# Moving the index path of a sparse attention beside the input projection, and its last top-k into the attention

## The reference

```python
(cq, k_att, v_att, k_idx, w_idx, q_m, k_m, v_m, o_m, i_m, f_m) = split(h @ w_in)   # 256, 512, 512, 64, 8, 4 x 512, 4, 4
cq = rms_norm_2(cq, q_latent_norm)
q = rope(cq @ w_q_up)            # 8 heads of 64
q_idx = rope(cq @ w_qidx_up)     # 8 index heads of 64
k, k_idx = rope(k_att), rope(k_idx)
# per block of 128 queries:
idx_score = sum over the 8 index heads of relu(q_idx . k_idx) * w_idx    # causal
sel = top_k(idx_score, 128)
att = softmax attention of q over the selected keys
# then an mLSTM on q_m, k_m, v_m, o_m, i_m, f_m, the product with w_out, and a SwiGLU
```

## Time and profile before

| | us |
|---|---|
| median of 3 runs | 3909.8 (3907.99 to 3910.78) |
| profiled execution, its own time | 3912.18 |
| its span | 3910.4 |
| PE busy / DVE busy / ACT busy / POOL busy, of the span | 90% / 45% / 28% / 0% |
| mean granted clock of TensorE | 0.932 of full |
| DMA queue of SP, share of 16 engines | 27.6% |

### The profile page before, as it was taken

The page is one execution under the profiler, slowest core; times in us unless marked ns, Lnnn a source line. Parts: engine busy times, 40 slices in busy tenths (PEclk is TensorE's granted clock), DMA queues, the critical chain, the costliest instruction groups (busy, mean ns, idle before and its releaser), DMA issues. The chain is left out here.

```text
span 3910.4 us, 49122 instructions
## 1 busy us (share of the span) xinstructions
PE 3521.6 (90%) x20384; PEld 2898.7 (74%) x20384; DVE 1753.6 (45%) x3310; ACT 1092.7 (28%) x1782; POOL 10.7 (0%) x12
## 2 busy tenths in 40 slices
PE   6998999999999988999998974799999983799997
PEld 5987677888887976878876963468887872568886
DVE  3225554333334235644344447653333448654333
ACT  3112443111113222532223222531222322533222
POOL 0000000000000000000000000000000000000000
PEclk9996999999999987999999995899999996799999
DMA  5440102423331210144442310026443320013332
GB/s 191 128 151 1 47 23 63 130 97 99 108 115 44 76 55 26 34 149 149 148 143 91 92 53 0 1 71 194 146 143 113 87 77 0 1 44 92 97 97 70
DMA packets 318717, 336.52 MB, mean 86 GB/s; under 512 B 12024, under 2 KB 233760, under 8 KB 318496
## 3 DMA queue, kind: packets, MB, share of 16 engines
q1 hardware_dynamic: 318496, 333.38, 27.6%
HBM read 329.67 MB, written 3.67 MB: 85 GB/s over the span
## 5 line engine op out<-in xcount | busy, mean ns | idle before, releaser
L1528 DVE TENSOR_TENSOR weights_low<-weights,weights_high 128x1024 fp32r<-128x1024 f32 (+4 forms) x424 | 485.7, 1148 | 1211.3 <-ACT weights_high L1155 1209.5
L1155 ACT ACTIVATE weights_high<-weights 128x1024 fp32r<-128x1024 f32 (+4 forms) x424 | 421.3, 996 | 1383.7 <-PE banks L580 956.2
L987 PE MATMUL banks<-h_high,weights_high 128*128 128x512 f32 (+1 forms) x1760 | 659.8, 375 | 10.1 <-DVE h_low L1540 6.0
L987 PE MATMUL banks<-h_low,weights_high 128*128 128x512 f32 (+1 forms) x1760 | 650.8, 370 | 0.0
L987 PE MATMUL banks<-h_high,weights_low 128*128 128x512 f32 (+1 forms) x1760 | 649.5, 369 | 0.0
L580 PE MATMUL banks<-weights_high,h_high 128*128 128x426 f32 (+3 forms) x1424 | 519.0, 364 | 4.2 <-DVE h_low L1540 4.2
L580 PE MATMUL banks<-weights_high,h_low 128*128 128x426 f32 (+3 forms) x1424 | 510.4, 358 | 0.0
L580 PE MATMUL banks<-weights_low,h_high 128*128 128x426 f32 (+3 forms) x1424 | 509.7, 358 | 0.0
L987 PEld LDWEIGHTS banks<-h_high,weights_high 128*128 128x128 f32 x1760 | 333.3, 189 | 79.3 <-issue 18.4
L987 PEld LDWEIGHTS banks<-h_high,weights_low 128*128 128x128 f32 x1760 | 333.4, 189 | 56.4
L987 PEld LDWEIGHTS banks<-h_low,weights_high 128*128 128x128 f32 x1760 | 333.7, 190 | 51.6
(11 more groups left out here) (257 smaller groups left out, 3908.2 us busy)
## 6 DMA issues: line engine op xcount, KB each, us to landing
projected<-in_w_mod SPq DMA_DIRECT2D x80, 1024.0 KB, 5.3
weights<-in_w_gate_up SPq DMA_DIRECT2D x88, 512.0 KB, 3.9
weights<-in_w_down SPq DMA_DIRECT2D x80, 512.0 KB, 3.7
weights<-in_w_in SPq DMA_DIRECT2D x80, 426.0 KB, 3.4
weights<-in_w_gate SPq DMA_DIRECT2D x44, 512.0 KB, 6.5
weights<-in_w_up SPq DMA_DIRECT2D x44, 512.0 KB, 6.3
weights<-in_w_mod SPq DMA_DIRECT2D x32, 512.0 KB, 3.8
weights<-in_w_out SPq DMA_DIRECT2D x32, 512.0 KB, 3.6
```

The source lines that it names most:

```text
L987: mm = pe.matmul(bank[:, 0:cnt], wt[:, k, :], x[:, k, a:a + cnt], start=(k == 0 and q == 0), stop=(k == KD - 1 and q == 2))
L1155: act.activation(WH[s_ % 2][:, 0:k * n], slots[j % LAND][:, 0:k * n], ACT.Copy).then_inc(S["w_high"], 1)
L1528: dve.tensor_tensor(WL[s_ % 2][:, 0:k * n], slots[split_of[s_] % LAND][:, 0:k * n], WH[s_ % 2][:, 0:k * n].bitcast(F32), ALU.subtract).the ...
```

## The change

The two layers of the second kind are reordered in five ways; the arithmetic is the same.

1. The columns of w_in are reordered on the host: cq, index keys, index weights and gates come first (336 columns), then keys, values and the mLSTM's four. The projection has 7 chunks, of 336 and six times 512 columns: 28 slots. ACT copies all of its banks (`keeps`).
2. The index path moves beside the projection. PE does, in its side banks behind the unit of the slot: the turns of cq (slot 6), of the index keys (7), the products with w_qidx_up for tiles 1 to 3 (8, 9), the turns of the index queries (11 to 13), the index scores of tile 1 (14, 15: eight matmuls of 256 keys), of tile 2 (16 to 19: two heads each) and of tile 3 (20 to 23). DVE does the norm of cq (4, 5), the rope of index keys (6) and index queries (10 to 12), the sums of tile 1 (15, 16), the 16 rounds of tile 1 (17 to 20, four each) and 15 rounds of tile 2 (22 to 26, three each; the last one behind the projection). ACT takes the relu, two a slot, in slots 15 to 24, into four buffers.
3. POOL takes over: the rope of the keys (four tiles), the weighted sums of tiles 2 and 3 (16 heads, a scale and an add each), and the rope of the queries (four tiles, six instructions of 128x256 each), in that order.
4. After the projection are left: the product with w_q_up, the turns of keys and queries, and the attention.
5. The 16 rounds of tile 3 stand in DVE's list between the pairs of the attention: two rounds behind the `weigh` of each of pairs 0 to 7, the mask behind pair 8. PE no longer waits for `nearly_chosen`, and does 3 instead of 5 dummy matmuls there.

The diff, cut to its core:

```diff
-M_Q, M_K, M_V, M_O, M_I, M_F = 1352, 1864, 2376, 2888, 3400, 3404
+A_C, A_KI, A_WI, M_I, M_F = 0, 256, 320, 328, 332
+W_IN2_FIRST = 336
...
-        chunks = [(W // 8 * j, W // 8, IN_T) for j in range(8)]
+        chunks = [(0, W_IN2_FIRST, IN_T)] + [(W_IN2_FIRST + 512 * j, 512, IN_T) for j in range(6)]
...
+            if second and slot == 8:
+                cols(w["w_qidx_up"], 0, 512, 0, 2, split=False)
...
+                elif 16 <= slot < 24:                                  # PE
+                    n = 2 if slot < 20 else 3
+                    for h in (2 * (slot % 4), 2 * (slot % 4) + 1):
+                        bank = side.fill(pe, "a")
+                        pe.matmul(bank[:, 0:128 * (n + 1)], QIT[b:b + 64, n - 1, f, :], KIT[b:b + 64, 0:128 * (n + 1)],
+                                  start=True, stop=True).then_inc(S["side"], 1)
...
-                if second:
-                    pe.wait_ge(S["nearly_chosen"], 1)
-                    warm(5, 6)
-                else:
-                    warm(3, 6)
+                warm(3, 6)
...
+                pe.wait_ge(S["key_rope_pool"], 1)
                 for f in range(4):
                     turn_columns(lambda t: pr(t, A_K + 128 * f, 128), ["a"])
+                for n in range(LAT_T):
+                    pe.wait_ge(S["query_rope"], n + 1)
+                    bank = B.fill(pe, "a")
...
+                def rotate(x, n):                                      # POOL
+                    pool.tensor_tensor(t1, x1, s_, ALU.mult)
+                    step(pool.tensor_tensor(t2, x2, s_, ALU.mult))
+                    pool.tensor_tensor(x1, x1, c, ALU.mult)
+                    step(pool.tensor_tensor(x2, x2, c, ALU.mult))
+                    pool.tensor_tensor(x1, x1, t2, ALU.subtract)
+                    step(pool.tensor_tensor(x2, x2, t1, ALU.add))
...
+                        part = RL[g % 4][:, 0:nk]
+                        if h == 0:
+                            pool.tensor_scalar(total[:, 0:nk], part, WI[:, n, h:h + 1], None, ALU.mult)
+                        else:
+                            step(pool.tensor_scalar(part, part, WI[:, n, h:h + 1], None, ALU.mult))
+                            pool.tensor_tensor(total[:, 0:nk], total[:, 0:nk], part, ALU.add)
...
+                for n in range(LAT_T):
+                    pool.wait_ge(S["emptied_act"], n + 1)
+                    rotate(QQ[:, n, :], n)
+                    pool.sem_inc(S["query_rope"], 1)
...
+                if 4 <= q < 8:                                         # ACT, before relu q
+                    act.wait_ge(S["index_sum"], q // 2 - 1)
+                elif q >= 8:
+                    act.wait_ge(S["pool_sum"], q - 7)
+                kept(RL[q % 4][:, 0:n], bank[:, 0:n], 1.0, ACT.Relu)
...
+                elif 17 <= slot < 21:                                  # DVE
+                    choose(1, 4 * (slot - 17), 4 * (slot - 16))
...
+                elif 22 <= slot < 27:
+                    choose(2, 3 * (slot - 22), 3 * (slot - 21))
...
+                    if between:
+                        between(p)
...
+                def last_tile(p):
+                    if p < 8:
+                        choose(3, 2 * p, 2 * p + 2)
+                    elif p == 8:
+                        mask(3)
```

More of the change, by code:

```diff
@@ L321, in layer @@
                     unit(w["w_mod"][PT * k:PT * (k + 2), 512 * c:512 * (c + 1)].rearrange("(k p) n -> p k n", p=PT), 2, 512, split=False)
+            if second and slot == 8:
+                cols(w["w_qidx_up"], 0, 512, 0, 2, split=False)
     if second:
-        for n in ("w_q_up", "w_qidx_up"):
-            cols(w[n], 0, 512, 0, 2, split=False)
+        cols(w["w_q_up"], 0, 512, 0, 2, split=False)
     else:
@@ L518, in layer @@
     turn = "ad"
+    keeps = "aa" if second else turn
     def by_rows(f, bank, h):
@@ L1162, in modulate @@
                         bank = T.share(act)
-                        act.activation(HH[:, f, a:a + cnt], bank[:, 0:cnt], ACT.Identity, scale=AT[:, which, f, r:r + 1],
+                        act.activation(HH[:, f, a - GOFF:a - GOFF + cnt], bank[:, 0:cnt], ACT.Identity, scale=AT[:, which, f, r:r + 1],
                                        bias=MT[:, 2 * which, f, r:r + 1]).then_inc(S["h_high"], 1)
@@ new lines, in choose @@
+            def choose(n, r0, r1):
+                nk = 128 * (n + 1)
+                sums = SUMS[n][:, 0:nk]
+                if r0 == 0:
+                    if n > 1:
+                        dve.wait_ge(S["pool_sum"], 8 * (n - 1))
+                    step(dve.tensor_tensor(sums[:, nk - 128:nk], sums[:, nk - 128:nk], CN[:, C_CAU:C_CAU + 128], ALU.add))
+                for r in range(r0, r1):
+                    src = sums if r == 0 else WK[:, 0:nk]
+                    step(dve.max(m8, src))
+                    step(dve.match_replace(WK[:, 0:nk], m8, src, TAKEN))
@@ L1828, in _, with mask @@
+            def mask(n):
+                nk = 128 * (n + 1)
+                mk = MK[:, MKO[n]:MKO[n] + nk]
+                step(dve.tensor_scalar(mk, WK[:, 0:nk], TAKEN, NEG, ALU.is_gt, ALU.mult))
+                step(dve.tensor_tensor(mk[:, nk - 128:nk], mk[:, nk - 128:nk], CN[:, C_CAU:C_CAU + 128], ALU.add))
             for j, (a, n, tt) in enumerate(chunks):
@@ L1837, in _ @@
                         side.empty(dve, "a", "d")
-                    if second and (j, i) != (7, 3):
+                    if second:
                         beside_projection(j, i)
@@ L1842, in _ @@
                 for i, t in enumerate(tt):
-                    bank = PB6.empty(dve, turn[i % 2], "d")
+                    bank = PB6.empty(dve, keeps[i % 2], "d")
                     if bank is not None:
                         dve.tensor_copy(pr(t, a, n), bank[:, 0:n]).then_inc(S["kept_dve"], 1)
-            PB6.all_emptied(dve)
+            if not second:
+                PB6.all_emptied(dve)
             if start_loads:
```

345 lines of the change are left out of this document (203 added, 142 removed).

## The result

The changed kernel takes 3782.79 us (median of 4 runs, 3782.15 to 3783.39), the kernel before 3909.04 us (4 runs): a ratio of 0.9677, with a 95% interval of 0.966 to 0.9693. Forecast was 3789, 6 us more. The profiled span is 3780.4 us, 130.0 less than the 3910.4 of before.

What follows compares the result with a forecast made beforehand. DVE's chain of relu sums and selection was taken to bound the kernel between projection and attention. Per layer 89.9 - 9.0 - 1.4 + 2.6 - 21.5 = 60.6 us, 121.2 for two, from 3909.8 to 3789; range 3760 to 3835.

Steps and rivals of the forecast that it cites:

- five terms: Per layer: 89.9 us gained before the attention, 9.0 and 1.4 lost in it, 2.6 gained and 21.5 lost in the projection.
- Stage A: From the projection's last matmul to the attention's first turned pair: 120.4 us becomes 30.5, a gain of 89.9 a layer.
- Rival (a): Query ropes and index sums: POOL takes 1.4 us an instruction with strided reads; 3830 us; chance 15%.
- The estimate of 0.56 us: Query ropes: a POOL instruction of 256 takes 0.56 us, the four ropes are 4 us shorter, the sum 3781.
- Projection: Input projection, per layer: 2.6 us gained by reordered columns, 21.5 lost to PE's added index work, no new wait.
- POOL's sums: Index sums beside the projection: scale 1.0 and add 1.5 us, 2.5 a head, 5.0 of the 6.2 two heads have.
- Rival (c): Beside the projection: DVE and POOL exclude each other, splits wait in ten slots; 12 us a layer, 3813; chance 10%.
- Stages B and C together: Attention pairs 0 to 7 lose 9.0 us a layer with DVE as bound; pairs 8 to 15 lose 1.4.
- Clock in C: Attention pairs 8 to 15: clock taken as the mean of the two layers, since nothing changes there.
- Rival (b): Attention pairs 8 to 15: clock stays at 1.2 GHz throughout, 19 us above the mean, 3827; chance 12%.
- (d): Ropes and pairs 8 to 15: POOL is as fast as DVE and the clock rises with pair 8; 3768; chance 11%.
- (e): Projection: POOL's sums hold ACT, ACT's splits hold PE; slower than before, 3967 at three times the POOL prices; chance 2%.

## Why the prediction was right, point by point

The time was 6 us off, and the signs of all five terms were right. By its steps, per layer, forecast against measured (layer 3, layer 4):

- **Stage A**, forecast 30.5 us: 30.5 and 30.3. Inside it, POOL's instruction was put at 0.7 us between the bounds 0.42 and 1.0, and took 0.72; the tile 4.4 against 4.5; the last rope T + 21.0 against T + 21.4. What chose 0.7 over the copy's rate was that the earlier trace rows showed a copy beside DVE work; the trace now has the copy at 3.96 us again beside that work and the ropes at 0.72 without. Rival (a), POOL at 1.4 us, is out. The estimate of 0.56 us for 256 elements, worked out in proportion from the figure for 2048 in the Trainium skill (GPSIMD Engine Reference, section 3.1), was too low: the instruction took 0.72, and no run here has one of 2048 elements with two inputs. That the kernel came out near the 3781 us of that estimate is luck, from the terms below.
- **Projection**, forecast 18.9 us lost: 17.4 and 17.5. The columns were right: the matmul of 336 columns has its 0.154 us pitch. The scores took 9.8 where the earlier trace rows had given 10.0. Two terms were too high: the products with w_qidx_up took 4.3 and not 5.3, and the changes of operand some 2 and not 3.4; the turns, 3.8 and not 2.8, made up for a part. No wait of PE was foreseen and none came beyond the one at the start (1.9 us) that was there before (2.10).
- **POOL's sums**, forecast 1.0 and 1.5 us (scale and add) at 512 keys: 1.56 and 1.28. The total of 2.5 us a head became 2.8 undisturbed and 3.2 in the mean, since in every second head the scale began during a split of DVE and took 2.1 to 2.35. The shares were wrong too: the instruction with one tensor and a scalar per partition is the dearer one, though it reads one input less. The cover of four buffers was enough, and the run with two more instructions a head shows by how much.
- **Rival (c)**, DVE and POOL excluding each other beside the projection: the exclusion exists and cost PE no wait. In the changed kernel's layer 3, a POOL scale that began during a split (2273.81 to 2275.33), and a POOL add during which a split began:

```profile
2274.41 2.35 POOL L1209 TENSOR_SCALAR scratch<-scratch,small 128x512 f32<-128x512 f32 x1 [0.16 <-POOL scratch L1210]
...
2286.81 1.28 POOL L1210 TENSOR_TENSOR scratch<-scratch,projected 128x512 f32<-128x512 f32 x1
```

```profile
2287.29 1.89 DVE L1642 TENSOR_TENSOR weights_low<-weights,weights_high 128x1024 fp32r<-128x1024 f32 x1 [1.40 <-ACT weights_high L1248]
```

  The add ends at 2288.09, and the split 1.1 us behind it, at 2289.18; undisturbed a split is 1.23. Of the step that priced this rival, "every split waits for a POOL add (1.5) in ten slots, and uses up its 2.9 of slack where DVE is full", the wait was over-priced and the slack was not used up: the mean split was 1.30 us where an undisturbed one is 1.23, and PE's slots had room. It was mostly POOL that waited. The Trainium skill (SBUF — State Buffer, "Who interferes with whom") has the rule that a DVE instruction with two SBUF inputs contends with a GpSimd instruction that reads SBUF, and the trace agrees here too.
- **Stages B and C together**, forecast 9.0 + 1.4 = 10.4 us lost: 7.5 and 13.1, 10.3 in the mean. The sum was right and the parts were not, by three steps, and that it came out so close is in part luck: the three runs that leave the attention as it is had B and C together 2.3 us shorter in the mean. One: I counted eight pairs of DVE work between the turns of pair 0 and pair 8. DVE's chain, from its first copy at 2333.12 to its last round at 2367.3, is 34.2 us, close to the forecast's; but pair 8 turns 2.4 us before it ends, so B shows a loss of 5.3 and 6.1 and the rest falls in C. Two: a pair took 3.65 us with 128 keys and 4.1 with 256, where the forecast had 3.95 and 4.4; waits at the two ends made up for most of it. Three: **"Clock in C: as the mean of the two layers, since nothing here changes pairs 8 to 15"** is the step that did not hold in this execution. The clock returned to 2.4 GHz for good 52 and 48 us behind the turn of pair 0 (20 and 16 us into C), and before 41 and 25 us behind it (15 us into C, and 1 us ahead of it). C lost 2.2 and 7.0 us, 4.6 in the mean and not 1.4; of the 3.2 us between them 2.4 are the end of DVE's chain that falls in C, so the clock's part is about 0.8 us in the mean, less than C varies from run to run.
- **Rival (b)**, 1.2 GHz through the whole of C: out; **(d)**, the clock up with pair 8: out; **(e)**: its mechanism was built with three more POOL instructions a head, and then cost 25 us.
- What the forecast did not see at all: DVE stands idle for 30.7 us in stage A, next to the engine that it waits for. It named POOL as "late next" and did not ask whether the work had to be there.

**The clock of C, what is shown and what stays open.** I read the granted clock of each run in stretches of 1 us. In every run it was at 1.2 GHz by 7 us behind pair 0's turn (in the one with dummies in the pairs by 11 us), after a stage A at 1.00 as after one at 0.77. In the seven kernels that keep two rounds a pair (the dummies in the pairs left aside) it was back for good 35 to 54 us behind pair 0, which is 13 us into C in the mean of 14 layers. In the three with at most one round a pair it was back 24 to 35 us behind it, 4 us into C in the mean of 6. C's pairs with three blocks of keys go at 5.6 us at the lower clock and 3.4 at full, so 9 us more of it are some 3.5 us a layer. So PE's waits for DVE in B go with a later return in the mean. That they cause it isn't shown: the two groups touch at 35, the kernel before has no round in its pairs and was back at 41 and 25, layers of one execution differ by ten us and more, full work through stage A did not move the return, and the dummies in B brought one that did not last. What decides it within one kernel stays open.

## What to carry to other kernels

When a chain leaves the critical path, price what is late next, and then ask which engine is idle beside it: here DVE had 30.7 us free while POOL did at 0.72 us what DVE does at 0.42, and sixteen rounds that fitted there stood in a stage that they bound. Work that is spread between the steps of a pipeline should be one piece a step, small enough to stay under PE's own pace, and its first pieces belong ahead of the waits of their engine, not behind them. And where a stage's time is the clock's, don't book it as a constant: here the same eight pairs took 29.8 to 38.9 us from run to run and layer to layer.

## What the runs showed of the hardware

- Two-input instructions of DVE and POOL alternate where both read SBUF. In layer 3's slots 8 to 12 POOL's rope of the keys, 0.73 us an instruction alone, takes 0.80 to 0.92 beside DVE's rope, whose own 0.42 become 0.84 to 0.96; beside a split one takes 1.59 and 1.76. Beside `max` and `match_replace` it stays at 0.72.

```profile
2193.08 0.80 POOL L1185 TENSOR_TENSOR projected<-projected,scratch 128x256 f32<-128x256 f32 x1
```

```profile
2193.32 0.84 DVE L1706 TENSOR_TENSOR scratch<-scratch 128x256 f32<-128x256 f32 x1
```

- On POOL a product with one scalar per partition over 384 elements takes 1.24 us and over 512 1.56, an add of two tensors 1.01 and 1.28. A scale over 512 that begins during a split of DVE takes 2.1 to 2.35 us, though it reads one tensor only.
- PE busy for 24.32 of 25.40 us with the pairs' small matmuls (stage B with the rounds gone) had a granted clock of 0.60; in the run with dummies in stage A it was 1.00 there, and in the B behind it 0.62 in layer 3 and 0.56 in layer 4.
